# A decoder trunk in split single precision: one weight unit's three products interleaved, with one wait for both halves

## The chip, the cores and the metric

The kernel runs on one core of a Trainium2 chip. The metric is the device time of one execution in microseconds (us), as a median over executions; the profile is of one execution. TensorE is written PE (matrix products), its weight loads PEld, VectorE DVE, ScalarE ACT, GpSimd POOL and SyncE SP.

## The reference

Two pre-norm residual layers over 256 tokens of width 1024, everything in float32, weights included:

```python
for i in range(DEPTH):
    h = rms_norm(x, attn_norm[i])
    c_q, c_kv, k_r, q_d, k_d, v_d, g_mla, g_dil = split(h @ w_in[i])
    o_mla = latent attention of 8 heads, causal        # q, k, v from the low-rank latents
    o_dil = 24 heads in 3 dilated windows, combined by their softmax denominators
    merged = sigmoid(g_mla) * (o_mla @ w_br_mla[i]) + sigmoid(g_dil) * (o_dil @ w_br_dil[i])
    x = x + merged @ w_out[i]
    h = rms_norm(x, ffn_norm[i])
    x = x + (swiglu(h, ...) if i == 0 else top-2-of-8 experts of swiglu(h, ...))
    h = rms_norm(x, ple_norm[i])
    x = x + sigmoid(h @ ple_w_gate[i]) * (p[i] @ ple_w_proj[i])
return rms_norm(x, final_norm)
```

`swiglu` is (silu(h @ w_gate) * (h @ w_up)) @ w_down with an inner width of 3584. Layer 1 has eight experts of that size, so most of the weights, and most of the time, are theirs.

## The kernel before

All weights come from one array in device memory, `stream`, in the order in which they are used: 468 slabs of 1 MiB, each 128 partitions by 2048 floats. A slab is two units of 128x1024 floats, mostly two blocks of 128 rows by 512 columns. SP loads the slabs into a ring of six (`raw`, L375), each as soon as the slab that lay there has been split.

A float32 product is made of three products of a faster type. A weight unit is split into `hi`, the value rounded to that type (ACT, L539), and `lo`, the rest (DVE, L842: raw minus hi). Both lie in rings of four units. The activations are split in the same way (`l_hi`, `l_lo`). A unit's product is then l_hi x hi + l_lo x hi + l_hi x lo, accumulated in PSUM; l_lo x lo is left out. The function `unit` issues it on PE. The parts of the activations are the stationary operand (128x128, a weight load for each matmul) and the weights move through (512 columns for most units).

Three semaphores count units: `hi_done` (ACT has written a hi), `lo_done` (DVE has written a lo) and `used` (PE has finished the unit's last product). ACT waits for `used` before it overwrites a place of the ring, so it can be four units ahead of PE at most; DVE follows ACT, and does everything else of the vector engine in between, in an order written out by hand.

Units are numbered through the kernel; a layer of attention has 80, the dense feed-forward 84, each expert 84, the last part of each layer (`ple`) 10. Where 256 tokens are processed, a unit has two blocks of rows for two halves of the tokens, with l_hi and l_lo of each: 12 matmuls. An expert gathers its tokens (at most 128) with a one-hot product (`gather`, L1522), so its units have 6 matmuls, all into one PSUM bank. A step of an expert is 12 units: 4 for gate, 2 for down, 4 for up, 2 for down, with a transposition of the activated values (`turn`, L1530) in it. The gather for the next expert comes in the last step of an expert, ahead of its last two units:

```python
if gath is not None:
    pe.wait_ge(e_stev, ex + 1)
    gather(gath)
down(ub + 10, dyn, 1, fd == 0, fd == NF - 1)
```

ACT rounds the gathered tokens (L757) and DVE copies their rest (L1155) before either splits the units that follow. On DVE, the products with the sigmoid (`f_up`, L1056, in the dense part; `up`, L1176, in an expert) stand ahead of the split of the next step's first unit, and wait for the unit that ends the up part:

```python
split_to(ub + 12, dyn)
up(ch, ub + 9, dyn)
```

Of the kernel before, what the change touches and what calls it, by code (L numbers as in the profile page):

```python
# [22 lines left out]
P = 128  # L23
# [68 lines left out]
def trunk_kernel(nc, x, p, positions, attn_norm, q_norm, kv_norm, ffn_norm, router_w, router_b, ple_norm,  # L92
                 final_norm, stream, out):
    ctx = ExitStack()
    with ctx:
# [138 lines left out]
        ps = ctx.enter_context(nc.psum_tensor("ps", [P, 8, CH], F32))  # L234

        def sem(name):
            return ctx.enter_context(nc.semaphore(name))
# [3 lines left out]
        hi_done = sem("hi_done")  # L241
        lo_done = sem("lo_done")
        used = sem("used")
        LO0, US0 = 2 * RAW, RING
# [994 lines left out]
        def _(pe):  # L1239
            def unit(u, dyn, l_hi, l_lo, dims, k0, outs, c0, first, last):  # L1240

                nk, w = dims
                pe.wait_ge(hi_done, dyn + u + 1)
                wh = hi[:, u % RING, 0:nk * w].rearrange("p (k n) -> p k n", k=nk)
                wl = lo[:, u % RING, 0:nk * w].rearrange("p (k n) -> p k n", k=nk)
                for kk in range(nk):
                    for t, bank in enumerate(outs):
                        o = ps[:, bank, c0:c0 + w]
                        ah, al = l_hi[:, k0 + kk, P * t:P * t + P], l_lo[:, k0 + kk, P * t:P * t + P]
                        pe.matmul(o, ah, wh[:, kk, :], start=(first and kk == 0), stop=False)  # L1250
                        pe.matmul(o, al, wh[:, kk, :], start=False, stop=False)  # L1251
                pe.wait_ge(lo_done, dyn + u + 1 + LO0)
                for kk in range(nk):
                    for t, bank in enumerate(outs):
                        ins = pe.matmul(ps[:, bank, c0:c0 + w], l_hi[:, k0 + kk, P * t:P * t + P], wl[:, kk, :],  # L1255
                                        start=False, stop=(last and kk == nk - 1))
                ins.then_inc(used, 1)

            def cols(u, dyn, l_hi, l_lo, outs, w=CH, nku=2, units=4, ready=None):

                for h in range(units):
                    if ready and h % 2 == 0:
                        pe.wait_ge(ready[0], ready[1] + 2 + h)
                    unit(u + h, dyn, l_hi, l_lo, (nku, w), nku * h, outs, 0, h == 0, h == units - 1)
# [12 lines left out]
            def attn(i, dyn=0):  # L1277
# [25 lines left out]
                for c in range(2):  # L1303
                    n = 5 + c
                    evacuated(n - 2)
                    for h in range(2):
                        unit(b + U_UQ + 2 * c + h, dyn, latT_hi, latT_lo, (KQ, 192), 0,
                             (2 * (n % 2), 2 * (n % 2) + 1), 192 * h, True, True)
                for c in range(2):
                    n = 7 + c  # L1310
                    evacuated(n - 2)
                    unit(b + U_UKV + c, dyn, latT_hi, latT_lo, (KKV, CH), KQ, (2 * (n % 2), 2 * (n % 2) + 1), 0, True, True)
# [181 lines left out]
            for t in range(T):  # L1494
                for k in range(KD):
                    o = ps[:, 0, NE * t:NE * t + NE]
                    ah, al = hT_hi[:, k, P * t:P * t + P], hT_lo[:, k, P * t:P * t + P]
                    pe.matmul(o, ah, rw_hi[:, k, :], start=(k == 0), stop=False)
                    pe.matmul(o, ah, rw_lo[:, k, :], start=False, stop=False)
                    ins = pe.matmul(o, al, rw_hi[:, k, :], start=False, stop=(k == KD - 1))  # L1500
# [12 lines left out]
            with pe.Fori(0, npv) as q:  # L1513
# [77 lines left out]
                with pe.Fori(0, NE - 1) as e:  # L1591
                    dyn = e * UPE + dq
# [104 lines left out]
```

## Time and profile before

| | |
|---|---|
| time, median of 3 executions | 2067.19 us (2067.1 to 2077.89) |
| the profiled execution: its own time | 2077.89 us |
| its span, first to last instruction | 2076.2 us |
| mean granted TensorE clock | 0.951 of full |
| PE / DVE / ACT busy | 1960.6 / 1488.4 / 1233.8 us |
| slabs loaded by SP | 468 of 1024 KB |
| splits on ACT (L539) and on DVE (L842) | 936 each |

A profile row of the timeline gives start, duration, engine, line, what is written and read, and a count where like instructions are merged; in brackets, idle time of the engine before it and what ended that. Matmuls overlap: their own duration (0.39 us) is longer than the distance between two starts, and it is the distance that counts. A granted clock of 1.00 is 2.4 GHz, 0.50 is 1.2 GHz.

### The profile page before, as it was taken

The page shows a single profiled execution, that of the slowest core. Times are in us where ns is not written, and L with a number is a line of the kernel's source. Part 1 is how long each engine was busy: PE and PEld are TensorE (multiplying, and loading weights), DVE is VectorE, ACT ScalarE, POOL GpSimd, SP SyncE. Part 2 cuts the span into 40 slices and gives each one's busy share as a digit, 9 for nine tenths or more (in the row PEclk, how much of TensorE's full clock was granted, in tenths as well). Part 3 has the DMA queues.
Part 4 walks back from the last instruction along what each step waited for, and adds up shares of the span by engine and source line. Part 5 has one row for each costly group of instructions (what it writes and reads, how often), then busy time and mean ns, then how long its engine had stood idle before and what let it go on. Part 6 is the DMA issues. An engine that isn't in the chain of part 4 may idle for free.

```text
span 2076.2 us, 27666 instructions
## 1 busy us (share of the span) xinstructions
PE 1960.6 (94%) x9278; PEld 1641.1 (79%) x9278; DVE 1488.4 (72%) x1659; ACT 1233.8 (59%) x1533; POOL 77.8 (4%) x131
## 2 busy tenths in 40 slices
PE   7998998999977998999799999999999999999996
PEld 6887887888866887877688888888888888888874
DVE  5455545566645455445499999989999898999974
ACT  5544444444434545334377887777878777887763
POOL 3100001000001300001000000000000000000001
PEclk9998789999988999779699999999999999999998
DMA  7642123545533543114299898989989999898970
GB/s 290 209 162 82 41 81 137 203 182 185 193 138 132 203 164 120 42 44 180 79 356 370 345 368 344 360 342 357 373 341 367 345 360 362 347 371 345 358 300 31
DMA packets 69760, 498.61 MB, mean 240 GB/s; under 512 B 7824, under 2 KB 7824, under 8 KB 9792
## 3 DMA queue, kind: packets, MB, share of 16 engines
q1 hardware_dynamic: 68352, 493.39, 63.0%
q0 software_dynamic: 1344, 4.36, 0.7%
q8 instruction: 41, 0.67, 0.1%
q14 instruction: 23, 0.19, 0.0%
HBM read 496.67 MB, written 1.05 MB: 240 GB/s over the span
## 4 chain that ended last, share of the span: by engine, by line
PE 92%; DVE 3%; ACT 2%; issue 1%; POOL 1%; DMA 1%; DVEq 0%; SPq 0%; ACTq 0%; POOLq 0%
PE ps L1250 27%; PE ps L1251 27%; PE ps L1255 27%; PE ps L1387 2%; PE ps L1522 2%; PE ps L1369 1%; PE ps L1530 1%; DVE lo L842 1%; PE ps L1335 1%; PE ps L1271 1%; PE ps L1380 1%; DMA raw<-in_stream 1%; PE ps L1358 1%; PE ps L1360 0%; ACT pT L642 0%
## 5 line engine op out<-in xcount | busy, mean ns | idle before, releaser
L842 DVE TENSOR_TENSOR lo<-raw,hi 128x1024 fp32r<-128x1024 f32 (+1 forms) x936 | 1104.0, 1220 | 235.5 <-ACT hi L539 234.7
L539 ACT ACTIVATE hi<-raw 128x1024 fp32r<-128x1024 f32 (+1 forms) x936 | 969.1, 1054 | 405.3 <-PE ps L1255 394.8
L1250 PE MATMUL ps<-hi,hs_hi 128*128 128x512 f32 x896 | 356.2, 398 | 2.1 <-ACT hi L539 2.1
L1250 PE MATMUL ps<-hi,hT_hi 128*128 128x512 f32 (+1 forms) x832 | 342.2, 413 | 10.7 <-DVE hT_lo L876 6.1
L1251 PE MATMUL ps<-hi,hs_lo 128*128 128x512 f32 x896 | 350.1, 391 | 0.0
L1251 PE MATMUL ps<-hi,hT_lo 128*128 128x512 f32 (+1 forms) x832 | 335.0, 404 | 0.0
L1255 PE MATMUL ps<-lo,hs_hi 128*128 128x512 f32 x896 | 276.9, 390 | 1.1 <-DVE lo L842 1.1
L1255 PE MATMUL ps<-lo,hT_hi 128*128 128x512 f32 (+1 forms) x832 | 224.8, 394 | 0.6 <-DVE lo L842 0.6
L1250 PEld LDWEIGHTS ps<-hi,hT_hi 128*128 128x128 f32 x832 | 165.7, 199 | 46.7 <-DVE hT_lo L876 8.1
L1255 PEld LDWEIGHTS ps<-lo,hs_hi 128*128 128x128 f32 x896 | 168.4, 188 | 37.8 <-DVE lo L842 1.5
L1250 PEld LDWEIGHTS ps<-hi,hs_hi 128*128 128x128 f32 x896 | 168.9, 188 | 35.5 <-ACT hi L539 2.2
L1251 PEld LDWEIGHTS ps<-hi,hs_lo 128*128 128x128 f32 x896 | 168.9, 189 | 33.3
L1251 PEld LDWEIGHTS ps<-hi,hT_lo 128*128 128x128 f32 x832 | 166.3, 200 | 32.8
L1255 PEld LDWEIGHTS ps<-lo,hT_hi 128*128 128x128 f32 x832 | 159.8, 195 | 35.1 <-DVE lo L842 1.1
L1250 PE MATMUL ps<-hi,eaT_hi 128*128 128x512 f32 x448 | 176.3, 394 | 2.9 <-DVE eaT_lo L1226 2.9
L1251 PE MATMUL ps<-hi,eaT_lo 128*128 128x512 f32 x448 | 175.3, 391 | 0.0
L1255 PE MATMUL ps<-lo,eaT_hi 128*128 128x512 f32 x448 | 138.4, 390 | 0.0
L632 ACT ACTIVATE pr<-pr,nmax 128x384 f32<-128x384 f32 (+2 forms) x64 | 39.1, 611 | 135.8 <-DVE o_dil L987 105.3
L1250 PEld LDWEIGHTS ps<-hi,eaT_hi 128*128 128x128 f32 x448 | 84.5, 189 | 22.7 <-DVE eaT_lo L1226 3.1
L1255 PEld LDWEIGHTS ps<-lo,eaT_hi 128*128 128x128 f32 x448 | 84.4, 188 | 17.9
L1251 PEld LDWEIGHTS ps<-hi,eaT_lo 128*128 128x128 f32 x448 | 84.6, 189 | 16.9
L986 DVE RECIPROCAL rsum<-sums 128x1 f32<-128x1 f32 (+2 forms) x44 | 7.3, 165 | 109.1 <-PE ps L1387 90.6
(259 smaller groups left out, 1845.5 us busy)
## 6 DMA issues: line engine op xcount, KB each, us to landing
raw<-in_stream SPq DMA_DIRECT2D x468, 1024.0 KB, 5.0
xs<-in_x SPq DMA_DIRECT2D x1, 1024.0 KB, 4.8
gain<-in_ffn_norm POOLq DMA_DIRECT2D x2, 512.0 KB, 6.3
gain<-in_ple_norm POOLq DMA_DIRECT2D x2, 512.0 KB, 4.4
out_x<-hnat SPq DMA_DIRECT2D x2, 512.0 KB, 2.9
gain<-in_attn_norm SPq DMA_DIRECT2D x1, 512.0 KB, 5.9
pnat<-in_p POOLq DMA_DIRECT2D x2, 256.0 KB, 4.4
gain<-in_attn_norm POOLq DMA_DIRECT2D x1, 512.0 KB, 3.6
```

The source lines that it names most:

```text
L539: a.activation(dst, src, ACT.Copy).then_inc(hi_done, 1)
L632: ins = a.activation(v, v, ACT.Exp, bias=nmax[:, n % 2, h:h + 1], accum_out=sums[:, n % 2, h:h + 1])
L842: v.tensor_tensor(dst, src, h, ALU.subtract).then_inc(lo_done, 1)
L1250: pe.matmul(o, ah, wh[:, kk, :], start=(first and kk == 0), stop=False)
L1251: pe.matmul(o, al, wh[:, kk, :], start=False, stop=False)
L1255: ins = pe.matmul(ps[:, bank, c0:c0 + w], l_hi[:, k0 + kk, P * t:P * t + P], wl[:, kk, :], start=False, stop=(last and kk == nk - 1))
L1271: ins = pe.transpose(ps[:, 4 + j, P * k:P * k + P], src[:, t, CH * h + P * k:CH * h + P * k + P], ident[:])
L1335: ins = pe.transpose(ps[0:m, 4 + 2 * (r % 2) + t, P * k:P * k + P], src[t][k], ident[:])
L1358: pe.matmul(o, qh, kh, start=True, stop=False)
L1369: ins = pe.transpose(ps[:, 4 + k // 4, P * (k % 4):P * (k % 4) + P], pr[:, n % 2, P * k:P * k + P], ident[:])
L1387: ins = pe.matmul(ps[:, 6, 0:64], pT[:, n % 2, (t + 1) * m + k, :], vd[:, k, hd:hd + 64], start=(m == 0 and k == 0), stop=(m == DG - 1 and ...
L1522: ins = pe.matmul(ps[:, banks[k // 4], P * (k % 4):P * (k % 4) + P], src[:, t, P * k:P * k + P], sel[:, t, :], start=(t == 0), stop=(t == ...
```

## The change

The two loops of `unit` become one. For each block of rows and each half of the tokens, the three products stand together: l_hi x hi, l_hi x lo, l_lo x hi, so that the first two, next to each other, have the same stationary operand. The wait for `hi_done` ahead of the unit goes, the wait for `lo_done` moves from the middle of the unit to its head, and the increment of `used` stands on the last matmul as before. Number, shape and operands of the matmuls and weight loads stay the same, and nothing changes on the other engines.

```diff
             def unit(u, dyn, l_hi, l_lo, dims, k0, outs, c0, first, last):
 
                 nk, w = dims
-                pe.wait_ge(hi_done, dyn + u + 1)
+                pe.wait_ge(lo_done, dyn + u + 1 + LO0)
                 wh = hi[:, u % RING, 0:nk * w].rearrange("p (k n) -> p k n", k=nk)
                 wl = lo[:, u % RING, 0:nk * w].rearrange("p (k n) -> p k n", k=nk)
                 for kk in range(nk):
@@
                         o = ps[:, bank, c0:c0 + w]
                         ah, al = l_hi[:, k0 + kk, P * t:P * t + P], l_lo[:, k0 + kk, P * t:P * t + P]
                         pe.matmul(o, ah, wh[:, kk, :], start=(first and kk == 0), stop=False)
-                        pe.matmul(o, al, wh[:, kk, :], start=False, stop=False)
-                pe.wait_ge(lo_done, dyn + u + 1 + LO0)
-                for kk in range(nk):
-                    for t, bank in enumerate(outs):
-                        ins = pe.matmul(ps[:, bank, c0:c0 + w], l_hi[:, k0 + kk, P * t:P * t + P], wl[:, kk, :],
-                                        start=False, stop=(last and kk == nk - 1))
+                        pe.matmul(o, ah, wl[:, kk, :], start=False, stop=False)
+                        ins = pe.matmul(o, al, wh[:, kk, :], start=False, stop=(last and kk == nk - 1))
                 ins.then_inc(used, 1)
```

## Rows read from the trace of the kernel before

**Rows 1.** The page: PE's busy time, its busy tenths and clock in 40 slices.
```profile
PE 1960.6 (94%) x9278; PEld 1641.1 (79%) x9278; DVE 1488.4 (72%) x1659; ACT 1233.8 (59%) x1533; POOL 77.8 (4%) x131
...
PE   7998998999977998999799999999999999999996
...
PEclk9998789999988999779699999999999999999998
```

**Rows 2.** The page: the chain that ended last, by line.
```profile
PE ps L1250 27%; PE ps L1251 27%; PE ps L1255 27%; PE ps L1387 2%; PE ps L1522 2%; PE ps L1369 1%; PE ps L1530 1%; DVE lo L842 1%; PE ps L1335 1%; PE ps L1271 1%; PE ps L1380 1%; DMA raw<-in_stream 1%; PE ps L1358 1%; PE ps L1360 0%; ACT pT L642 0%
```

**Rows 3.** Windows: stretch, busy time of PE, PEld, DVE, ACT, POOL; clock, DMA share.
```profile
360.00:363.50 3.50, 3.50 (x8) 2.76 (x9) 3.50 (x4) 2.68 (x3) 0.00 (x0) 0.50 0.34 97
...
1025.50:1029.00 3.50, 3.46 (x8) 2.79 (x9) 3.48 (x4) 3.32 (x4) 0.00 (x0) 0.50 0.00 0
...
1043.00:2008.00 965.00, 965.00 (x4491) 801.13 (x4490) 898.12 (x880) 752.22 (x805) 0.00 (x0) 1.00 0.94 358
```

**Rows 4.** Groups by line, 1150 to 2000 us: busy us, mean ns, idle before.
```profile
L842 DVE TENSOR_TENSOR lo<-raw,hi 128x1024 fp32r<-128x1024 f32 x580 | 677.6, 1220 | 30.3 <-ACT hi L539 30.3
```

**Rows 5.** Waits of PE, whole span: total us, times, longest.
```profile
PE ps L1255 <- DVE lo L842: 1.7, 2, 1.1
```

**Rows 6.** Timeline of an ordinary expert unit.
```profile
1408.24 0.39 PE L1250 MATMUL ps<-hi,eaT_hi 128*128 128x512 f32 x1
...
1408.46 0.39 PE L1251 MATMUL ps<-hi,eaT_lo 128*128 128x512 f32 x1
...
1409.60 0.39 PE L1250 MATMUL ps<-hi,hs_hi 128*128 128x512 f32 x1
```

**Rows 7.** Timeline behind the gather for the second expert.
```profile
1143.25 4.84 ACT L539 ACTIVATE hi<-raw 128x1024 fp32r<-128x1024 f32 x5
...
1144.34 4.63 DVE L842 TENSOR_TENSOR lo<-raw,hi 128x1024 fp32r<-128x1024 f32 x4 [0.78 <-ACT hi L539]
...
1144.74 0.19 PEld L1250 LDWEIGHTS ps<-hi,hs_hi 128*128 128x128 f32 x1
1144.96 0.39 PE L1250 MATMUL ps<-hi,hs_hi 128*128 128x512 f32 x1
```

**Rows 8.** Timeline, first expert's second step: PE stopped in a unit's middle.
```profile
1038.57 0.69 DVE L1176 TENSOR_TENSOR e_act<-e_sig,ps 128x512 f32<-128x512 f32 x1 [2.04 <-PE ps L1255]
...
1039.18 4.62 DVE L842 TENSOR_TENSOR lo<-raw,hi 128x1024 fp32r<-128x1024 f32 x4
1040.45 0.30 PEld L1255 LDWEIGHTS ps<-lo,hs_hi 128*128 128x128 f32 x2 [1.52 <-DVE lo L842]
1040.45 0.73 PE L1255 MATMUL ps<-lo,hs_hi 128*128 128x512 f32 x2 [1.10 <-DVE lo L842]
1040.79 0.19 PEld L1250 LDWEIGHTS ps<-hi,hs_hi 128*128 128x128 f32 x1
```

**Rows 9.** Timeline, dense part's second step: the same.
```profile
384.89 5.76 DVE L842 TENSOR_TENSOR lo<-raw,hi 128x1024 fp32r<-128x1024 f32 x5
...
386.17 1.20 PE L1255 MATMUL ps<-lo,hT_hi 128*128 128x512 f32 x4 [0.64 <-DVE lo L842]
```

**Rows 10.** Timeline at the first unit of the dense part and of the experts.
```profile
359.87 2.36 DVE L842 TENSOR_TENSOR lo<-raw,hi 128x1024 fp32r<-128x1024 f32 x2 [0.25 <-ACT hi L539]
...
359.98 0.76 PE L1250 MATMUL ps<-hi,hT_hi 128*128 128x512 f32 x1 [1.72 <-ACT hi L539]
...
1025.52 4.63 DVE L842 TENSOR_TENSOR lo<-raw,hi 128x1024 fp32r<-128x1024 f32 x4 [0.78 <-ACT hi L539]
...
1025.54 0.80 PE L1250 MATMUL ps<-hi,hs_hi 128*128 128x512 f32 x1 [2.06 <-ACT hi L539]
```

**Rows 11.** Timeline, dilated scores: L1358 and L1359 share their stationary operand.
```profile
854.85 0.28 PE L1358 MATMUL ps<-qk_hi 64*128 64x256 f32 x1
854.97 0.28 PE L1359 MATMUL ps<-kT_lo,qk_hi 64*128 64x256 f32 x1
855.09 0.28 PE L1360 MATMUL ps<-qk_hi,qT_lo 64*128 64x256 f32 x1
```

## The prediction

> **What bounds the kernel now.** I read the page first. PE is busy for 94% of the span [rows 1], and its slices show 9 almost without a break from slice 21 on, where the experts are; at the borders of the stages it falls to 7 or 8 and the clock with it. The chain that ended last runs 27% + 27% + 27% over the three product lines of `unit` [rows 2], in equal thirds, as their numbers of instructions are. Then the windows: from 1043 to 2008 us PE has no idle time at all, at clock 1.00, while DVE is busy 898 of 965 us (93%) and the DMA engines are at 0.94 [rows 3]. So PE is the bound there, with DVE and the loads close behind: whatever delays PE by one microsecond in the experts lengthens the kernel by one, and nothing later gives it back.
>
> How fast PE goes: two matmuls of a unit start 0.22 to 0.23 us apart, and a unit of six takes 1.36 us from its first start to the next unit's (1408.24 to 1409.60), so 0.227 each [rows 6]. That is 512 columns at 2.4 GHz (0.213) and 0.013 more.
>
> The waits of PE: in the whole kernel it stopped only twice for a `lo`, for 1.7 us together [rows 5]. This is the number that the change puts at risk, as today four of six matmuls (eight of twelve) can run before `lo` is asked for. So I went through all 936 units in the timeline and compared the end of each unit's split on DVE with the start of its first matmul, for the change asks that the first be over before the second. In nearly all units it is, mostly by 0.3 to 1.5 us in the experts and by more elsewhere. It isn't in 20. Those fall into three kinds, which are the terms below.
>
> **The change part by part.**
>
> *Order of the matmuls.* Their number and shapes stay. The three of a group now write the same bank one after another; in the experts all six do so already, at 0.227 each [rows 6], and that is the full pace of this kernel. Cost: nothing. The second of a group now repeats the stationary operand, but its weight load is still issued: there are as many loads as matmuls, 9278 of each [rows 1], though this kernel has such repeats already. These are in the dilated scores: L1358 and L1359 share their stationary operand, L1360 has another, and both distances are 0.12 us at 256 columns [rows 11], which is 0.107 plus the same 0.013. Gain: nothing. The bounds are 0 and 0.013 us for each of some 2400 groups (two in each of the 672 expert units, four in most of the other 264), 32 us; I take 0, as the nearest row shows none.
>
> *The `hi_done` wait goes.* DVE can make a `lo` only from a finished `hi`, so the later wait covers it. One wait fewer in each unit; PE's starts show no seam at either wait where it is met in time (1.36 us is six times 0.227) [rows 6]. Gain: nothing.
>
> *The `lo_done` wait moves to the head.* Nothing on PE can pass it, so what is queued behind is the whole unit and all after it, and behind those ACT's next `hi`, which waits for `used`.
>
> (a) Behind a gather. ACT rounds the gathered tokens before it splits on, so its look-ahead is used up. ACT's next split starts at 1143.25, DVE's at 1144.34, and with 1.22 us for one split on DVE [rows 4] that `lo` is there at 1145.56, whereas PE started the unit at 1144.96 [rows 7]: 0.60 us late. A restart costs more than the lateness. Where PE really stopped for a `lo` [rows 8], the split begun at 1039.18 (1.22) ended at 1040.40, PE's weight load and matmul both started at 1040.45, and the second followed after 0.34 instead of 0.227 (a weight load starts as the matmul before it does: 1040.45, 1040.79). So 0.05 us for the signal and 0.11 for a weight load that nothing covers. One stall costs 0.60 + 0.16 = 0.76 us. The next unit's `lo` was 0.38 late, and by then PE is 0.76 later itself, so it costs nothing more. The pattern stands seven times, every 124 us, with the same numbers: 7 x 0.76 = 5.3 us. From below: 7 x 0.60 = 4.2.
> The Trainium skill ("TensorE: Matmul & The Clock Gate", Step-by-step, ①) says that PE pulls weight loads ahead of matmuls in flight. Here rows 8 show the load held back by the wait as well; by the rule alone the 0.11 would go, and the sum would be 0.8 us less.
>
> (b) Where PE already stops in mid-unit. At 1039.18 and at 384.89 DVE begins the `lo` only after a product that waits for PE's unit just ended (L1176 idle 2.04 us <- PE) [rows 8]. PE used that time for its `hi` products. Restart in the middle at 1040.45 becomes restart at the head at the same moment, so the matmuls done before are moved behind: 4 x 0.227 = 0.91 us there, and 8 x 0.227 = 1.82 at 386.17 in the dense part, where a unit has twelve [rows 8, 9]. Together 2.7 us, a firm term.
>
> (c) The first unit of a feed-forward part, where PE waits for the splits to begin at all. `lo` ends at 1025.52 + 1.22 = 1026.74 against a start at 1025.54, and at 359.87 + 1.22 = 361.09 against 359.98 [rows 10]. With 0.05 each: 1.25 and 1.16, 2.4 us. The clock is at its lower level just behind both starts (0.50 from 1025.5 to 1029 and from 360 to 363.5) [rows 3]. If it rises at the same moment as now, PE loses half-speed time, and the term is half, 1.2 us; if it rises as much later as PE starts later, the term is whole. I take it whole. The Trainium skill (same page, Part 1) says that the slow level is the default and that activity lifts it, which speaks for the whole term; no row here shows a moved start.
>
> (d) The clock behind (b). PE's stops there grow from 1.10 to about 2.0 us and from 0.64 to 2.5. A stop of this length has no row of its own amid full work; much longer ones at stage borders end in the lower clock [rows 1, 3]. If the clock drops for a stretch like those of rows 3 (3.5 us at 0.50), PE loses 1.75 us each time. From 0 to 3.5 us; I take 1.75, one of two.
>
> Everywhere else the added wait costs nothing, covered by splits that are ahead: the ring lets ACT and DVE run up to four units ahead, and four are 5.4 us of PE. SP waits for `lo_done` only and is as far ahead as before.
>
> Sum: 5.3 + 2.7 + 2.4 + 1.75 = 12.2 us. Lower 4.2 + 2.7 + 1.2 + 0 = 8.1, upper 5.3 + 2.7 + 2.4 + 3.5 = 13.9. The profiled execution took 2077.89 us, 10.7 above the median of the three; none of the terms depends on what made it longer, so it would be 2090, and on the median's scale 2067.2 + 12.2 = 2079.4 us, 0.6% slower. A change of under 0.5%, 10.3 us, can hardly be told from none by a measurement of this kernel, and my sum lies only just beyond.
>
> **The rivals.**
>
> *R1, faster: the repeated stationary operand pays.* If the second load of a group were free in truth, some 2400 groups would save up to 0.013 us, 32 us, less the 12 of the stalls: 2047 us. It decides from 0.005 us a group on. For it: PE is 0.013 above its column time, and the loads are the natural suspect. Against it: rows 11, where a repeat gains nothing. The Trainium skill (same page, Back-to-back issue gap) gives 216 ns for an isolated matmul of 512 columns and counts the load apart; by it some 11 ns would be to be had, 26 us. The trace has 227 and no case of 216.
>
> *R2, no change that can be measured.* The stalls are there, but a part is taken back: (c) is halved by the clock, (d) doesn't occur, and PE's later stops at the end of the dense part (PE waits for DVE there anyway) swallow some of (b). Then 4.2 to 5.3 plus some 2 to 3: 2073 us. For it: only (a) lies in a stretch without any idle PE. Against: those later waits are for work that itself follows from PE's.
>
> *R3, clearly slower: DVE can't hold the tighter date.* DVE is at 93% in the experts and now must deliver 0.91 us (four matmuls) earlier. If one unit in each of the 56 steps were caught by 0.16 us (the restart alone), it would be 9 us more, 2088 us. For it: the smallest leads behind a gather are only some 0.2 us. Against it: in the ordinary steps PE's pace gives DVE more slack with every stall, for DVE's own work doesn't grow.
>
> **How the numbers follow.** My forecast (all of (a) and (b), most of (c), some of (d)): 0.50, between 2074 and 2083. R1: 0.05. R2: 0.28. R3: 0.12. Something else, either way: 0.05. The range 2070 to 2090 leaves out R1, the lowest part of R2 and the ends of the rest. Slower by over 0.5% (above 2077.5) is most of the forecast's case and R3: 0.58. Within 0.5%: R2 and the forecast's lower part, 0.36. Faster: 0.06.
>
> **What would show it.** In the changed kernel's trace, PE's waits for `lo` at the first product line should be about 11 (seven of 0.5 to 0.8 us, at 124 us distance, one near 2.0 and one near 2.5, two at the first units), where they were 2 for 1.7 us. From 1043 to 2008 PE should no longer be without idle time, and that stretch should be longer by some 5 us. The distance between matmuls should stay 0.227; a value near 0.22 for the second of a group would make R1 right. The clock just behind the two longest stops decides (d), and the moment of its rise behind the first expert unit decides (c). Many short waits in ordinary steps would be R3. I would be wrong altogether if the order of the products itself changed PE's pace.

## The result and the profile after

The changed kernel takes 2088.66 us (median of 5, 2079.76 to 2090.23) against 2070.2 us (median of 5, 2067.1 to 2077.89). The measured ratio of the executions is 1.0068, 95% interval 1.0038 to 1.0098; it is not the quotient of the two medians, which lie 18.5 us apart (1.009), and the ratios below are of the same kind. It is slower, by about 0.7%; the forecast was 0.6%. The profiled execution has a span of 2088.7 us, 12.5 longer than the 2076.2 of before.

The page after: PE's busy time, and its busy tenths and clock in 40 slices.

```profile
PE 1965.3 (94%) x9278; PEld 1644.2 (79%) x9278; DVE 1491.1 (71%) x1659; ACT 1235.8 (59%) x1533; POOL 77.1 (4%) x131
...
PE   7999998999977998999799999999999999999986
...
PEclk9997899999988999779699999999999999999998
```

Against [rows 1] the same number of matmuls and loads, and 4.7 us more busy time (1965.3 against 1960.6). So 7.8 of the 12.5 us are not in the matmuls but between them, and the slices are too coarse to show where. The waits of PE do (total us, times, longest):

```profile
PE ps L1250 <- DVE lo L842: 14.2, 11, 3.3
```

It was 1.7 us in 2 [rows 5]. The windows after, for the stretch of [rows 3] that had no idle PE and for the stretches behind the long stops (columns as there: clock, DMA share and GB/s last):

```profile
386.50:390.50 4.00, 4.00 (x13) 3.11 (x12) 2.20 (x2) 0.83 (x1) 0.00 (x0) 0.57 0.64 238
390.50:394.50 4.00, 4.00 (x23) 3.43 (x22) 1.22 (x1) 1.13 (x2) 0.00 (x0) 1.00 0.71 287
1029.50:1035.50 6.00, 6.00 (x15) 4.70 (x16) 4.55 (x4) 3.06 (x4) 0.00 (x0) 0.51 0.60 224
...
1045.50:1049.00 3.50, 3.50 (x9) 2.72 (x10) 3.23 (x3) 0.80 (x1) 0.00 (x0) 0.51 0.33 89
1043.00:2008.00 965.00, 959.53 (x4454) 795.52 (x4453) 893.66 (x873) 745.77 (x798) 0.00 (x0) 1.00 0.92 354
```

PE now has 5.5 us of idle time from 1043 to 2008, and the first stretch, just behind a stop, has a mean clock of 0.57 where the next has 1.00: for most of it the clock is at its lower level. (The counts, 13 and 23 matmuls in 4 us, exaggerate the difference, as 8 of the 23 are short transposes.)

The timeline after: the first unit of the dense part, its second step, the first expert unit, the first expert's second step, and behind a gather.

```profile
357.90 2.36 DVE L842 TENSOR_TENSOR lo<-raw,hi 128x1024 fp32r<-128x1024 f32 x2 [0.25 <-ACT hi L539]
...
359.28 0.57 PE L1250 MATMUL ps<-hi,hT_hi 128*128 128x512 f32 x1 [2.98 <-DVE lo L842]
...
384.07 3.49 DVE L842 TENSOR_TENSOR lo<-raw,hi 128x1024 fp32r<-128x1024 f32 x3
385.35 0.19 PEld L1250 LDWEIGHTS ps<-hi,hT_hi 128*128 128x128 f32 x1 [2.87 <-DVE lo L842]
385.35 0.50 PE L1250 MATMUL ps<-hi,hT_hi 128*128 128x512 f32 x1 [2.45 <-DVE lo L842]
...
1029.48 0.79 PE L1250 MATMUL ps<-hi,hs_hi 128*128 128x512 f32 x1 [3.32 <-DVE lo L842]
...
1045.38 0.65 PE L1250 MATMUL ps<-hi,hs_hi 128*128 128x512 f32 x1 [2.00 <-DVE lo L842]
...
1151.64 2.36 DVE L842 TENSOR_TENSOR lo<-raw,hi 128x1024 fp32r<-128x1024 f32 x2 [0.78 <-ACT hi L539]
...
1152.92 0.50 PE L1250 MATMUL ps<-hi,hs_hi 128*128 128x512 f32 x1 [0.49 <-DVE lo L842]
1153.26 0.40 PE L1251 MATMUL ps<-lo,hs_hi 128*128 128x512 f32 x1
```

Each is a stop at L1250, the unit's head, that ends some 0.05 us after a split on DVE (1151.64 + 1.22 = 1152.86, start at 1152.92); only the dense part's first takes 0.16. These rows stand against [rows 7 to 10]. The idle time of PE rose from 0.64 to 2.45 in the dense part's second step, from 1.10 to 2.00 in the expert's, from 1.72 to 2.98 and from 2.06 to 3.32 at the two first units, and from nothing to 0.49 behind each of seven gathers. The 11 waits are all there: 2.45 + 2.00 + 2.98 + 3.32 + 7 x 0.49 = 14.2. At 1152.92 the next matmul follows after 0.34, the weight load that nothing covers.

Between them PE's pace is unchanged. Two matmuls with the same stationary operand (L1250, L1251) and one with another (L1252), timeline after:

```profile
1175.78 0.39 PE L1250 MATMUL ps<-hi,eaT_hi 128*128 128x512 f32 x1
1176.00 0.39 PE L1251 MATMUL ps<-lo,eaT_hi 128*128 128x512 f32 x1
1176.23 0.39 PE L1252 MATMUL ps<-hi,eaT_lo 128*128 128x512 f32 x1
```

The time of one expert, between two starts of the unit behind a gather that lie six experts apart, is the cleanest measure, as the clock is 1.00 there. Before, from 1144.96 [rows 7] to 1888.36; after, from 1152.92 (above) to 1900.48. The last starts, first of before, then of after:

```profile
1888.36 0.39 PE L1250 MATMUL ps<-hi,hs_hi 128*128 128x512 f32 x1
```

```profile
1900.48 0.50 PE L1250 MATMUL ps<-hi,hs_hi 128*128 128x512 f32 x1 [0.49 <-DVE lo L842]
```

743.40 against 747.56 us: an expert takes 123.90 before and 124.59 after, 0.69 more.

Where the 12.5 us of the profiled pair lie, by distances between first matmuls of units (us); a part's tenth unit starts where its first nine end:

| stretch | before | after | more |
|---|---|---|---|
| to the first unit of the dense part | 359.98 | 359.28 | -0.7 |
| its first nine units (359.98 to 387.20; 359.28 to 389.44) | 27.22 | 30.16 | 2.9 |
| from there to the first expert unit | 638.34 | 640.04 | 1.7 |
| the experts' first nine units (to 1041.02; from 1029.48 to 1047.96) | 15.48 | 18.48 | 3.0 |
| from there to the first gather's unit | 103.94 | 104.96 | 1.0 |
| six experts | 743.40 | 747.56 | 4.2 |
| the rest of the span | 187.8 | 188.2 | 0.4 |

The rows with 2.9, 3.0, 1.0 and 4.2 hold the nine stops in mid-stream and most of what the clock added, 11.1 us together. The longer waits ahead of the two first units (1.26 each) and the last 0.4 us of the clock's loss behind the dense part's stop lie in the first and the third row, which else are mostly attention. They should make these rows 2.9 us longer, and the rows are 1.0 longer. The 1.9 us between can't be put down to the change, as executions of the same code differ there by more: the third row is 640.0 us here and 633.4 in the kernel below with only the gathers cured, whose code is the same up to the last step of the first expert. What makes them differ is open.

### The profile page after: what moved, and what is told of

The parts are those of the page before. It is cut to its first block, busy times and chain, and to the rows that moved or that the text cites. A ratio compares the mean times of both kernels' runs of the same rounds, so it can differ in the third digit from the quotient of the medians.

```text
span 2088.7 us, 27383 instructions
## 1 busy us (share of the span) xinstructions
PE 1965.3 (94%) x9278; PEld 1644.2 (79%) x9278; DVE 1491.1 (71%) x1659; ACT 1235.8 (59%) x1533; POOL 77.1 (4%) x131
## 4 chain that ended last, share of the span: by engine, by line
PE 91%; DVE 4%; ACT 2%; issue 1%; POOL 1%; DMA 1%; DVEq 0%; ACTq 0%; SPq 0%; POOLq 0%
PE ps L1250 27%; PE ps L1251 26%; PE ps L1252 26%; DVE lo L842 2%; PE ps L1383 2%; PE ps L1518 2%; PE ps L1365 1%; PE ps L1526 1%; PE ps L1331 1%; PE ps L1267 1%; PE ps L1376 1%; ACT hi L539 1%; DMA raw<-in_stream 1%; PE ps L1354 1%; PE ps L1343 0%
## 5 line engine op out<-in xcount | busy, mean ns | idle before, releaser
L1250 PE MATMUL ps<-hi,hs_hi 128*128 128x512 f32 x896 | 357.9, 399 | 8.8 <-DVE lo L842 8.8
L1250 PE MATMUL ps<-hi,hT_hi 128*128 128x512 f32 (+1 forms) x832 | 340.6, 409 | 14.1 <-DVE hT_lo L876 5.9
L1252 PE MATMUL ps<-hi,hs_lo 128*128 128x512 f32 x896 | 351.3, 392 | 0.0
L1251 PE MATMUL ps<-lo,hs_hi 128*128 128x512 f32 x896 | 350.7, 391 | 0.0
L1251 PE MATMUL ps<-lo,hT_hi 128*128 128x512 f32 (+1 forms) x832 | 333.3, 401 | 0.0
L1252 PE MATMUL ps<-hi,hT_lo 128*128 128x512 f32 (+1 forms) x832 | 332.6, 400 | 0.0
L1250 PEld LDWEIGHTS ps<-hi,hs_hi 128*128 128x128 f32 x896 | 169.4, 189 | 45.4 <-DVE lo L842 12.4
L1250 PEld LDWEIGHTS ps<-hi,hT_hi 128*128 128x128 f32 x832 | 164.4, 198 | 49.9 <-DVE hT_lo L876 5.7
L1252 PEld LDWEIGHTS ps<-hi,hs_lo 128*128 128x128 f32 x896 | 169.2, 189 | 36.7
L1251 PEld LDWEIGHTS ps<-lo,hs_hi 128*128 128x128 f32 x896 | 169.6, 189 | 33.5
L1252 PEld LDWEIGHTS ps<-hi,hT_lo 128*128 128x128 f32 x832 | 164.1, 197 | 35.0
L1251 PEld LDWEIGHTS ps<-lo,hT_hi 128*128 128x128 f32 x832 | 164.5, 198 | 32.3
L1250 PE MATMUL ps<-hi,eaT_hi 128*128 128x512 f32 x448 | 175.6, 392 | 2.9 <-DVE eaT_lo L1226 2.9
L1251 PE MATMUL ps<-lo,eaT_hi 128*128 128x512 f32 x448 | 175.0, 391 | 0.0
L1252 PE MATMUL ps<-hi,eaT_lo 128*128 128x512 f32 x448 | 175.0, 391 | 0.0
L1250 PEld LDWEIGHTS ps<-hi,eaT_hi 128*128 128x128 f32 x448 | 84.5, 189 | 20.5 <-DVE lo L842 3.2
L1252 PEld LDWEIGHTS ps<-hi,eaT_lo 128*128 128x128 f32 x448 | 84.5, 189 | 17.9
L1251 PEld LDWEIGHTS ps<-lo,eaT_hi 128*128 128x128 f32 x448 | 84.5, 189 | 17.4
```

The costliest lines, as they stand in the source:

```text
L1251: pe.matmul(o, ah, wl[:, kk, :], start=False, stop=False)
L1252: ins = pe.matmul(o, al, wh[:, kk, :], start=False, stop=(last and kk == nk - 1))
```

## The experiments

Two theories. The stall theory: the loss comes from where PE asks for `lo`, and is the sum of the lateness of some splits, with what the clock adds. The order theory: the order of the products changes PE's own pace, for good (a repeated stationary operand) or bad. All ratios below are against the kernel before, run on the same chip.

**The wait alone.** The order of the products is that of before (lines against the kernel before).

```diff
-                pe.wait_ge(hi_done, dyn + u + 1)
+                pe.wait_ge(lo_done, dyn + u + 1 + LO0)
...
-                pe.wait_ge(lo_done, dyn + u + 1 + LO0)
                 for kk in range(nk):
                     for t, bank in enumerate(outs):
                         ins = pe.matmul(ps[:, bank, c0:c0 + w], l_hi[...], wl[:, kk, :], ...)
```

> The wait alone: the products stay in the order of before (all with hi, then all with lo), but the wait for lo stands at the unit's head. Stall theory (the loss comes from asking for lo before the first product): the same waits as the changed kernel, 11 for about 14 us, and the same time, 0.4 to 1.0% above before. Order theory (interleaving or the repeated stationary operand itself costs PE time): no slower than before.

2081.61 us, ratio 1.006 (1.0044 to 1.0076). Its waits for `lo`, and its first and last start behind a gather:

```profile
PE ps L1250 <- DVE lo L842: 14.2, 11, 3.3
```

```profile
1144.34 0.50 PE L1250 MATMUL ps<-hi,hs_hi 128*128 128x512 f32 x1 [0.49 <-DVE lo L842]
...
1891.83 0.50 PE L1250 MATMUL ps<-hi,hs_hi 128*128 128x512 f32 x1 [0.49 <-DVE lo L842]
```

The same 14.2 us in 11 waits, and 747.49 / 6 = 124.58 us for an expert, within 0.01 of the changed kernel. Within the intervals the moved wait makes the whole of the loss; in an expert, where the traces are sharpest, the order adds nothing to it.

**The order without the wait.** One repeat of the stationary operand in each unit, across the old wait (lines against the kernel before; `pairs` lists the unit's blocks and banks in their order).

```diff
-                        pe.matmul(o, ah, wh[:, kk, :], start=(first and kk == 0), stop=False)
-                        pe.matmul(o, al, wh[:, kk, :], start=False, stop=False)
+                    for a in ((al, ah) if (kk, t, bank) == pairs[-1] else (ah, al)):
+                        pe.matmul(o, a, wh[:, kk, :], start=(first and kk == 0 and a is ah), stop=False)
                 pe.wait_ge(lo_done, dyn + u + 1 + LO0)
-                for kk in range(nk):
-                    for t, bank in enumerate(outs):
+                for kk, t, bank in reversed(pairs):
```

> The order without the wait: hi_done at the head and lo_done in the middle as before, but the last group of the hi products is issued l_lo, l_hi and the lo products run in reverse, so that the stationary operand is repeated once in each unit across the middle. Stall theory: 2 waits for lo, the time of before within 0.3%. If a repeated stationary operand paid (R1): 936 x 0.013 = 12 us less, and a distance near 0.214 us ahead of the first lo product. If it cost: more than before.

2072.18 us, ratio 1.0009 (0.9991 to 1.0026): no difference. Its waits, and its timeline at one unit, where L1251 is a hi product and L1254 a lo product:

```profile
PE ps L1254 <- DVE lo L842: 1.7, 2, 1.1
```

```profile
1136.63 0.39 PE L1251 MATMUL ps<-hi,hs_hi 128*128 128x512 f32 x1
1136.85 0.62 PE L1251 MATMUL ps<-hi,hs_lo 128*128 128x512 f32 x2
1137.31 0.39 PE L1251 MATMUL ps<-hi,hs_hi 128*128 128x512 f32 x1
1137.53 0.62 PE L1254 MATMUL ps<-lo,hs_hi 128*128 128x512 f32 x2
```

From 1137.31 to 1137.53 the stationary operand stays the same, and the distance is the usual 0.22 to 0.23. An expert takes (1879.99 - 1136.63) / 6 = 123.89 us, as before. A repeat that gave or cost 0.013 us in each of the 84 units of an expert would make 1.1 us, which would be seen here.

**Between the two.** Two matmuls ahead of the wait instead of four (or eight) before and none after (lines against the changed kernel).

```diff
-                pe.wait_ge(lo_done, dyn + u + 1 + LO0)
+                pe.wait_ge(hi_done, dyn + u + 1)
...
                         pe.matmul(o, ah, wh[:, kk, :], start=(first and kk == 0), stop=False)
-                        pe.matmul(o, ah, wl[:, kk, :], start=False, stop=False)
-                        ins = pe.matmul(o, al, wh[:, kk, :], start=False, stop=(last and kk == nk - 1))
+                        pe.matmul(o, al, wh[:, kk, :], start=False, stop=False)
+                        if kk == 0 and t == 0:
+                            pe.wait_ge(lo_done, dyn + u + 1 + LO0)
+                        ins = pe.matmul(o, ah, wl[:, kk, :], start=False, stop=(last and kk == nk - 1))
```

> Between the two kernels: the groups stay interleaved, but the two hi products of the first group come before the wait for lo, so that two matmuls are out of its way instead of four (or eight) before and none after. Stall theory, from 0.60 us lateness plus 0.05 for the signal less 2 x 0.227: 0.2 us for each of seven gathers (1.4), 2 x 0.227 = 0.45 at the first expert's second step, 6 x 0.227 = 1.36 in the dense part, 0.3 to 0.4 at each first unit at the lower clock: 4 us in all and perhaps one drop of the clock (1.7), so 0.2 to 0.3% above before. Order theory: as slow as the changed kernel.

2078.04 us, ratio 1.0037 (1.0022 to 1.0052): between the two kernels, at the upper edge of what I expected or a little above. Its timeline behind the first gather, and the last start:

```profile
1144.29 0.39 PE L1250 MATMUL ps<-hi,hs_hi 128*128 128x512 f32 x1
1144.52 0.39 PE L1251 MATMUL ps<-hi,hs_lo 128*128 128x512 f32 x1
1144.95 0.50 PE L1254 MATMUL ps<-lo,hs_hi 128*128 128x512 f32 x1
1145.29 0.39 PE L1250 MATMUL ps<-hi,hs_hi 128*128 128x512 f32 x1
...
1889.08 0.39 PE L1250 MATMUL ps<-hi,hs_hi 128*128 128x512 f32 x1
```

The third matmul comes 0.43 after the second, 0.20 late, as worked out; then 0.34 instead of 0.227, the uncovered load that I had left out of this expectation. An expert takes 744.79 / 6 = 124.13 us, 0.23 more than before. So the price in an expert follows the number of matmuls ahead of the wait: 0 for four, 0.23 us for two, 0.69 for none.

**The lateness taken away at its source.** The changed kernel's `unit` is kept. In the last step of an expert, ACT and DVE split two more units ahead of their work on the gathered tokens, while PE is still at the gather; and in the first step of the dense part and of the first expert DVE splits two units ahead of the product that waits for PE.

```diff
 # ACT, and the same on DVE ahead of gather_copy (first kind)
                     if gath is not None:
+                        split_to(ub + 14, dyn, dr)
                         gather_round(gath)
 # DVE (second kind), here the first expert; likewise ahead of f_up()
                 gate_up(ch)
+                split_to(b + 10, dq)
                 up(ch, b + 7, dq)
```

First both kinds together:

> The changed kernel with the lateness taken away at its source: ACT and DVE split the two units that follow a gather before they round and copy the gathered tokens, and DVE splits two more units before the product that waits for the up part in the first step of the dense part and of the first expert. Stall theory: the seven waits of 0.65 us and the two of 2.2 to 3.3 us are gone, only the two at the first units are left; 0.1 to 0.2% above before (2 to 4 us), and from 1043 to 2008 PE is without idle time again. Order theory: as slow as the changed kernel, 0.7% above before. Third way: the earlier splits delay the gathered tokens, and PE waits for hs_hi or hs_lo instead.

2074.01 us, ratio 1.0021 (1.0005 to 1.0038). Its waits for `lo`, its window without idle PE, and the first and last start behind a gather:

```profile
PE ps L1254 <- DVE lo L843: 6.3, 2, 3.3
```

```profile
1035.00:2000.00 965.00, 965.00 (x4496) 803.19 (x4495) 902.20 (x880) 755.77 (x806) 0.00 (x0) 1.00 0.93 358
```

```profile
1137.63 0.39 PE L1254 MATMUL ps<-hi,hs_hi 128*128 128x512 f32 x1
...
1880.38 0.39 PE L1254 MATMUL ps<-hi,hs_hi 128*128 128x512 f32 x1
```

Nine of the eleven waits are gone, the two at the first units stay, and PE is again without idle time in 965 us. An expert takes 742.75 / 6 = 123.79 us. The gathered tokens do not hold PE up. Most of the loss is cured without touching the order of the products or the place of the wait.

Then each kind alone:

> The changed kernel with only the splits behind a gather made earlier (two units split before the gathered tokens are rounded and copied). Stall theory: the seven waits of 0.65 us (0.50 of them shown as idle) go, and an expert takes 123.8 to 123.9 us instead of 124.59 (before 123.90); the four other waits for lo stay, about 10.7 us in all shown for them. Time 0.4% above before. Rival (the gathers' stalls are covered by something else): an expert stays at 124.6.

2080.2 us, ratio 1.0044 (1.0024 to 1.0064). An expert takes 123.79 us (1143.60 to 1886.35), and the waits left are the four others:

```profile
PE ps L1252 <- DVE lo L843: 10.7, 4, 3.3
```

> The changed kernel with only the splits in the two first steps made earlier. Stall theory: the two waits of 2.45 and 2.0 us in the first steps go, the drop of the clock that followed the longer of them goes too, and an expert stays at 124.59 us. From the first unit of the dense part to the tenth: 26 us (30.2 with the stall and the drop, 27.2 before); the same in the first expert: 15 us (18.5, 15.5 before). Time 0.3% above before. Rival: the clock drops there whatever the stall.

2079.18 us, ratio 1.0048 (1.0028 to 1.0067), nearer 0.5% than the 0.3% expected, with the lower edge at it. The trace does what was said: the waits left are nine, an expert takes 124.61 us (1138.35 to 1885.99), the first nine units take 385.11 - 359.17 = 25.9 us in the dense part and 14.8 in the first expert. The clock is 1.00 around its second step:

```profile
PE ps L1252 <- DVE lo L842: 9.7, 9, 3.3
```

```profile
380.00:390.00 10.00, 10.00 (x50) 8.38 (x49) 4.76 (x5) 4.15 (x5) 0.00 (x0) 1.00 0.56 198
```

The two cures add up within their intervals: from 1.0068, one takes off 0.0024 and the other 0.0020, both together 0.0047.

**How near DVE is.** The changed kernel, but in the experts' steps each unit waits at its head for the next unit's `lo`.

```diff
-                pe.wait_ge(lo_done, dyn + u + 1 + LO0)
+                pe.wait_ge(lo_done, dyn + u + 1 + ahead + LO0)      # ahead = 1 in step(), 0 elsewhere
```

> How near DVE is (R3): the changed kernel, but each unit of the experts' steps waits for the lo of the next unit at its head, one unit (1.36 us) earlier than it needs it. Between the end of a unit and the lo that takes its place in the ring lie 0.3 + 1.06 + 1.2 = 2.5 us, and two units of PE are 2.7: ordinary splits would just be in time, each of DVE's other operations of 0.6 to 0.7 us (three or more in a step) would not. Theory that the lead is what protects the kernel: some 1 to 2 us for each of 56 steps, 2070 + 60 to 120 us, 3 to 6% slower. Rival (DVE has enough slack at 93%, and only the special places stall): under 1% slower than before.

2192.91 us, ratio 1.0607 (1.056 to 1.0654). Its first and last start behind a gather, and its longest waits from 1158 to 1988 us:

```profile
1158.00 0.39 PE L1250 MATMUL ps<-hi,hs_hi 128*128 128x512 f32 x1
...
1987.82 0.39 PE L1250 MATMUL ps<-hi,hs_hi 128*128 128x512 f32 x1
```

```profile
ACT hi L539 <- PE ps L1252: 166.2, 342, 2.1
PEld ps L1250 <- DVE lo L842: 98.8, 147, 2.3
DVE lo L842 <- ACT hi L539: 72.8, 166, 1.3
```

An expert takes 829.82 / 6 = 138.3 us, 13.7 more than the changed kernel's, which is 2.0 us for each of its seven steps. Some 0.85 us of the 13.7 is the clock, which falls to 0.50 for some 3.4 us behind three of these stops (last section). So asking 0.9 us earlier (four matmuls) costs 0.7%, and asking another 1.36 us earlier costs 5.4% more. The changed kernel stands just ahead of that edge, not on it: R3 did not happen in it, and its mechanism is real one unit further.

**The kernel before with the same earlier splits.** The version that could beat both.

> The kernel before, with both kinds of earlier splits, as the version that could beat both. Stall theory: its only two waits for lo (1.7 us) go, the clock in the dense part can't drop there, and the rest is as before: 2 us, 0.1% faster, within what a measurement can tell. An expert 123.8 us. Rival: the earlier splits hold up the gathered tokens or the products and cost something: an expert over 123.9.

2070.22 us, ratio 0.9985 (0.9963 to 1.0006). No wait for `lo` is left, and an expert takes (1884.50 - 1141.70) / 6 = 123.80 us, 0.10 less than before. That is not in the waits for `lo`, of which an expert behind the first gather had none; the explanation may be the 0.09 us of the next section. The gain that the trace shows, some 2 us, is too small for the times to tell.

## Why the prediction was right

*What bounds, and the pace.* Right. PE stays the bound, and the expert's time went up by what PE waited. PE's pace is 0.227 per matmul in either order, so 0 was right for the order and for the repeated stationary operand; R1 is excluded by the wait alone (as slow as both parts), by the order alone (no gain) and by the three distances above.

*(a), 5.3 us forecast.* Seven stalls, each with 0.05 for the signal and the uncovered load, as worked out. An expert is 0.69 longer, not 0.76. The unit starts 0.66 later against the one ahead of it and takes 1.49 us instead of 1.36, 0.79 together; 0.09 comes back sixteen units later: before, the down part there began with a distance of 0.29 instead of 0.227 (timeline of before),

```profile
1167.70 0.46 PE L1250 MATMUL ps<-hi,eaT_hi 128*128 128x512 f32 x1
1167.99 0.40 PE L1251 MATMUL ps<-hi,eaT_lo 128*128 128x512 f32 x1
```

and after it has the usual one (1175.78 to 1176.00, above): PE is later by then, and something that it had just waited for is ready. No run isolates what that is; the rest of a down operand from DVE (L1185, `eaT_lo`) is the candidate. In the kernel before it ends at 1167.44 and the down part's first weight load starts at 1167.65, 0.2 us behind it; after, it ends at 1175.32 and the load starts at 1175.55, where the matmuls' own pace puts it. In the kernel before with earlier splits the distance is the usual one too (1164.43 to 1164.66). Seven times 0.69 is 4.8 us. At a stop the load is held back with the matmul (385.35 for both; at 1152.92, 0.34 to the next), so loads pulled ahead of matmuls in flight (the Trainium skill, "TensorE: Matmul & The Clock Gate", Step-by-step, ①) don't reach across a wait here; the measurement decides.

*(b), 2.7 us forecast.* Exact in its mechanism: the restarts came 0.05 after the same splits, and the idle time rose by 1.81 and 0.90 us.

*(c), 2.4 us forecast, in the whole.* The idle time rose by 1.26 at both first units, 2.5 us. At the dense part the clock rose as long behind the start as before (mean clock of the 5 us behind it: 0.64 before, 0.66 after), so the term is whole there. But I had left the clock at two cases, the rise at the same moment or as much later as PE starts. At the first expert unit it came later than both, which added about 1 us (below).

*(d), 1.75 us forecast as one of two drops.* In the profiled execution both happened: some 3.4 us at 0.50 behind either stop (the windows above, 0.57 over 4.0 us and 0.51 over 3.5), which costs half of that each time, 3.4 us together. Over the kernels that have these stops, the drop behind the longer one (2.45 us) is in the changed kernel, in the wait alone and in the gather cure; in the one-unit-earlier kernel the low clock of the part's start reached to 367 us, and there was none behind the stop. The drop behind the shorter (2.00 us) is in the changed kernel, but not in the wait alone and not in the gather cure. Without the stops it is in none. So one of two is about right; the profiled execution had both.

*The sum.* 4.8 + 2.7 + 2.5 + 3.4 + 1 = 14.4 us, against 12.5 in the profiled pair, whose attention happened to be 1.9 shorter than the terms would have it, and against 14 us by the ratio (0.68%; 18.5 by the medians alone). The forecast of 12.2 was short by the clock's part: 1.75 for what came to 4.4 in this execution. That it came so near is partly luck, since the clock differs between executions (0.949 to 0.956 of full on average over those of the changed kernel), and the measured interval, 0.4 to 1.0%, holds sums from 8 to 20 us.

*The rivals.* R2, no measurable change, is excluded for this comparison only just (the interval begins at 0.4%); the wait alone, with the same stops, has a narrower one, 0.44 to 0.76%. Its conditions failed too in the profiled execution: (c) was not halved, and (d) occurred. R3 did not occur: no ordinary step has a wait for `lo`.

## What to carry to other kernels

A wait moved from the middle of a block to its head costs, at each place, the lateness of what it waits for, up to the work that used to run under it; both can be read from the trace of before, by setting the end of every producer instruction against the start of the first consumer. Averages don't show it (from 1043 to 2008 us DVE was at 93% both times, and PE at 100% before and 99% after): 11 places of 936 made the loss, each next to something else that the producer has to do in its written order, and nine of them were cured there. And a stall of an engine whose clock follows its activity can cost more than its length.

## What the hardware showed

At the first expert unit the clock rose later behind a start that came later. This unit finds PE at the low clock. Window from 4.2 to 5.0 us after PE's first matmul of that unit, first in the kernel before (start 1025.54), then in the wait alone (start 1022.80):

```profile
1029.74:1030.54 0.80, 0.80 (x5) 0.65 (x4) 0.80 (x2) 0.24 (x1) 0.00 (x0) 1.00 0.71 297
```

```profile
1027.00:1027.80 0.80, 0.80 (x4) 0.61 (x3) 0.80 (x1) 0.00 (x0) 0.00 (x0) 0.50 0.99 420
```

The same window reads 1.00 in all four kernels in which PE starts with hi products (before, the order alone, two matmuls ahead of the wait, before with earlier splits), and 0.50 in all six in which it waits for `lo` first (the changed kernel, the wait alone, the three kernels with earlier splits and the changed unit, one unit earlier). PE's idle time ahead of the start is 2.06 us in the former and 3.32 in the latter. The extra low stretch costs half of its length. The Trainium skill ("TensorE: Matmul & The Clock Gate", Part 1) has the slow level as the default that activity lifts, which agrees.

At the first unit of the dense part, where the idle time ahead goes from 1.72 to 2.98 us, this order does not show. The same window behind that start, in the order alone (start 355.82, hi products first) and in the wait alone (start 359.05, `lo` first):

```profile
360.02:360.82 0.80, 0.80 (x3) 0.61 (x3) 0.32 (x1) 0.00 (x0) 0.00 (x0) 0.50 0.80 338
```

```profile
363.25:364.05 0.80, 0.80 (x5) 0.67 (x4) 0.00 (x0) 0.36 (x1) 0.00 (x0) 1.00 0.92 389
```

So that a later start delays the rise is shown at one place only, and why is open.

Nor does the length of a stop alone decide whether the clock falls behind it. Over the profiled executions it fell for some 3.4 us behind stops of 2.45 us in three of four, and of 2.00 us (or 1.99, in the dense part of the kernel between the two) in one of four. In the one-unit-earlier kernel it fell behind three of the seven stops of 1.87 us at the gathers, and not behind one of 3.14 us in the first expert's second step:

```profile
1431.58 0.50 PE L1250 MATMUL ps<-hi,eaT_hi 128*128 128x512 f32 x1 [1.87 <-DVE lo L842]
1041.14 0.50 PE L1250 MATMUL ps<-hi,hs_hi 128*128 128x512 f32 x1 [3.14 <-DVE lo L842]
```

```profile
1432.50:1435.50 3.00, 3.00 (x9) 2.32 (x8) 1.78 (x3) 1.06 (x1) 0.00 (x0) 0.50 0.51 153
1041.14:1047.14 6.00, 6.00 (x28) 4.82 (x28) 5.06 (x5) 3.56 (x4) 0.00 (x0) 1.00 0.79 294
```

Behind the stops of 0.49 us it stayed at 1.00.
